# Split weights stored as interleaved high and low elements instead of in separate tiles

## What the reference computes

```
proj = (x * (1 + sc1) + sh1) @ w_in + b_in         # 2048 -> q, three kv, gates, r_x, r_y, merge gates
o_attn = attention(q, kv, gates) @ w_attn_o        # compressed, selected and window branches
o_rnn  = (rg_lru(conv(r_x)) * gelu(r_y)) @ w_rnn_o
mix = (g_attn * o_attn + g_rnn * o_rnn) @ w_out
x = layer_norm(ALPHA * x + (1 + g1) * mix)
gt, up = split((x * (1 + sc2) + sh2) @ w_ffn_in)   # 2048 -> 2 * 5632
x = layer_norm(ALPHA * x + (1 + g2) * ((silu(gt) * up) @ w_ffn_out))
```

## Time and profile before

| | |
|---|---|
| three runs | 1770.25, 1773.12, 1779.43 us; median 1773.12 |
| profiled execution | 1772.58 us, of which the span from first to last instruction is 1770.9 us |
| TensorE busy with matmuls | 1733.3 us, 13514 matmuls |
| weight loads | 1598.4 us, 13514 loads |
| DVE, ACT busy | 899.8 us, 710.9 us |
| mean granted TensorE clock | 0.994 |

### The profile page before, as it was taken

One profiled execution on the slowest core, in us unless ns is written; L12 is line 12 of the kernel. 1 busy time (PEld: TensorE's weight loads), 2 busy tenths in 40 slices (PEclk: granted clock), 3 DMA queues, 4 the chain that ended last, 5 costly groups with the idle time before them and its releaser, 6 DMA issues.

```text
span 1770.9 us, 34473 instructions
## 1 busy us (share of the span) xinstructions
PE 1733.3 (98%) x13514; PEld 1598.4 (90%) x13514; DVE 899.8 (51%) x1632; ACT 710.9 (40%) x1076; POOL 157.0 (9%) x271
## 2 busy tenths in 40 slices
PE   8989999999999999999999999999999999999997
PEld 3558888888999999889988899999999999999997
DVE  2233346755656655565873344444444444444565
ACT  2222236764545443343563333333333333333344
POOL 0001312203332311100000000000000000000001
PEclk9999999999999999999999999999999999999998
DMA  9998878757655647985647854545555444544542
GB/s 341 374 384 303 304 258 282 290 212 259 191 181 177 207 150 277 352 317 179 212 147 261 291 208 165 166 129 165 164 190 183 164 168 161 169 152 140 165 165 75
DMA packets 114152, 384.05 MB, mean 217 GB/s; under 512 B 14942, under 2 KB 15326, under 8 KB 113663
## 3 DMA queue, kind: packets, MB, share of 16 engines
q1 hardware_dynamic: 103248, 349.82, 57.1%
q0 software_dynamic: 10208, 32.32, 5.5%
q10 hardware_dynamic: 590, 0.44, 0.1%
HBM read 373.48 MB, written 9.03 MB: 216 GB/s over the span
## 4 chain that ended last, share of the span: by engine, by line
PE 91%; DMA 5%; DVE 1%; ACT 1%; issue 1%; SPq 0%; POOL 0%; POOLq 0%; ACTq 0%; DVEq 0%
PE bank L722 26%; PE bank L723 25%; PE bank L724 25%; DMA raw<-in_w_units 4%; PE bank L729 3%; PE bank L769 3%; PE bank L747 2%; PE bank L895 1%; PE bank L1015 1%; PE bank L931 1%; DMA mgate<-mg 0%; ACT z L1518 0%; PE bank L962 0%; DVE wlo L385 0%; SPq L486 0%
## 5 line engine op out<-in xcount | busy, mean ns | idle before, releaser
L722 PE MATMUL bank<-xhi,wlo 128*128 128x288 f32 x2544 | 756.9, 298 | 2.4 <-DVE wlo L385 1.7
L723 PE MATMUL bank<-xlo,whi 128*128 128x288 f32 x2544 | 750.2, 295 | 0.0
L724 PE MATMUL bank<-xhi,whi 128*128 128x288 f32 x2544 | 748.6, 294 | 0.0
L385 DVE TENSOR_TENSOR wlo<-raw,whi 128x1024 fp32r<-128x1024 f32 (+2 forms) x468 | 510.1, 1127 | 373.1 <-ACT whi L377 366.2
L377 ACT CAST whi<-raw 128x1024 fp32r<-128x1024 f32 (+2 forms) x468 | 434.0, 969 | 419.1 <-PE bank L724 272.7
L722 PEld LDWEIGHTS bank<-xhi,wlo 128*128 128x128 f32 x2544 | 477.7, 188 | 15.7 <-issue 13.8
L723 PEld LDWEIGHTS bank<-xlo,whi 128*128 128x128 f32 x2544 | 478.4, 188 | 0.6
L724 PEld LDWEIGHTS bank<-xhi,whi 128*128 128x128 f32 x2544 | 478.7, 188 | 0.0
L722 PE MATMUL bank<-hhi,wlo 128*128 128x288 f32 x704 | 208.5, 296 | 0.0
L723 PE MATMUL bank<-hlo,whi 128*128 128x288 f32 x704 | 208.0, 295 | 0.0
L724 PE MATMUL bank<-hhi,whi 128*128 128x288 f32 x704 | 207.5, 295 | 0.0
(11 more groups left out here) (332 smaller groups left out, 1680.3 us busy)
## 6 DMA issues: line engine op xcount, KB each, us to landing
raw<-in_w_units SPq DMA_DIRECT2D x556, 512.0 KB, 6.0
raw<-in_w_ffn_out_units SPq DMA_DIRECT2D x64, 384.0 KB, 3.0
raw<-in_w_ffn_out_units SPq DMA_DIRECT2D x64, 320.0 KB, 3.4
raw<-in_w_units SPq DMA_DIRECT2D x16, 448.0 KB, 8.4
mgate<-mg POOLq DMA_DIRECT2D x32, 144.0 KB, 4.1
mgl<-mgate POOLq DMA_DIRECT2D x16, 288.0 KB, 7.1
bz<-relrow POOLq DMA_DIRECT2D x16, 192.0 KB, 3.3
xt<-in_x SPq DMA_DIRECT2D x8, 288.0 KB, 7.2
```

The lines of the kernel that those rows point to most:

```text
L385: nc.vector.tensor_tensor(wlo[e][:, part], raw[:, s, spot], f32(whi[e][:, part]), ALU.subtract).then_inc(raw_used[s][h], 1)
L722: pe.matmul(acc, wt[1][:, w], x[0][:, c, :], start=start, stop=False)
L723: pe.matmul(acc, wt[0][:, w], x[1][:, c, :], start=False, stop=False)
L724: return pe.matmul(acc, wt[0][:, w], x[0][:, c, :], start=False, stop=stop)
```

## The change

The two tiles of a buffer become one, twice as long: `wsplit0` and `wsplit1`, seen as 2048 pairs. The high part of an element is the first of its pair, the low part the second. `whi` and `wlo` are now views of these tiles that take every second element.

```diff
-        whi = [behind(ctx, f"whi{e}", (0, 64)[e], UNIT) for e in range(2)]
-        wlo = [behind(ctx, f"wlo{e}", (64, 32)[e], UNIT) for e in range(2)]
-        xhi = tokens(ctx, "xhi", 96, DC)
+        wsplit = [behind(ctx, f"wsplit{e}", (0, 64)[e], 2 * UNIT).rearrange("p (n s) -> p n s", s=2) for e in range(2)]
+        whi, wlo = ([w[:, :, s] for w in wsplit] for s in range(2))
+        xhi = tokens(ctx, "xhi", 64, DC)
         xlo = tokens(ctx, "xlo", 0, DC)
```

## The result

The changed kernel takes 1783.5 us in the median of four runs (1780.35 to 1784.95), the kernel before 1773.1 us: 1.0052 times the time, with a 95% interval of 1.0029 to 1.0074. It is slower by half a per cent, where 3.3% faster was forecast. The profiled execution took 1780.35 us with a span of 1778.7 us, 7.8 us more than that of before.

The account below looks back on a forecast made before the run. TensorE's matmul pitch on the split products was taken as the bound. From 1772.6 us, 57.7 us gained (59.9 less 2.2) gave 1714.9 us, all other terms nothing; whole range 1665 to 1870 us.

Parts of the forecast that it names:

- Load beside columns: Split-product matmuls: a stepped load keeps its distance from the columns, removing 5.7 ns of each pitch, 57.7 us gained.
- two readers that get into each other's way: Split products: column stream and weight load disturb each other at certain address distances, making the pitch's excess.
- The 11.5 ns: Split-product matmuls: part of the 132.1 ns pitch beyond 120.6 ns of column streaming.
- rival 1: Split products: the excess is a fixed cost, pitch 132.1 +- 0.8 ns, time 1764 to 1781 us; chance 0.18.
- the plain columns: Line 931, plain float32: 0.838 ns a column against 0.833 for two cycles, taken as next to no excess beside loads.
- rival 2: Split products: loads touching twice the memory cost up to 11.5 ns more, 1833 us at half that; chance 0.31.
- The count of matmuls: Lines 722 to 724 and 729: 10944 matmuls touched, one nanosecond on all worth 10.9 us; 10512 counted.
- The load's cover: Split-product matmuls: a stepped load slower by less than 24 ns is hidden by the streaming.
- rival 3: Split products: the load becomes the bound from 132 ns on; at twice 108 ns, 2656 us; chance 0.04.
- The signs: Trace after, if right: 125 to 129 ns per matmul, loads still 188 ns, steps varying less, gain after 137 us.
- The offsets: Split tiles: some stay at multiples of 128 bytes, high and low share one distance from the tokens; not priced.
- cover of three microseconds: ACT and DVE splits: a unit takes 3.3 us, the matmuls between 6.3 us, so slower stepped writes were priced at nothing.

Follow-up runs that it names:

- c1: Kernel before, lines 722 to 724 streaming 256 of the 288 columns except at the first block of each sum; 1659.2 us.
- c5: Kernel before, lines 722 to 724 loading 64 of the 128 weight columns except at the first and last block of each sum; 1765.2 us.
- e1: Changed kernel, but high and low parts alternate by blocks of 128 elements in the shared tile, so loads have no step; 1774.9 us, ratio 1.0012.
- e4: Kernel before, with high and low parts of both buffers in one tile, so a load reads every fourth element; 2875.9 us, ratio 1.6224.
- e5: Kernel before, separate tiles without a step, all split weight and token tiles at a multiple of 128 bytes; 1781.5 us, ratio 1.0054.
- e3: Changed kernel with its step, xhi and xlo moved to 16 bytes behind a multiple of 128; 1781.4 us, ratio 1.0050.
- e6: Changed kernel with its step, the two split tiles moved to 32 and 16 bytes behind a multiple of 128; 1781.6 us, ratio 1.0056.
- e7: Changed kernel with its step, the two split tiles moved to 96 and 80 bytes behind a multiple of 128; 1784.85 us, ratio 1.0063.
- e2: Kernel before, separate tiles without a step, high and low tiles of a buffer at the same offset; 1768.75 us, ratio 0.9974.
- c3: Kernel before, lines 722 to 724 streaming 128 of the 288 columns except at the first block of each sum; 2206 us.
- c4: Changed kernel, lines 722 to 724 streaming 128 of the 288 columns except at the first block of each sum; 1748 us.

## Why the prediction was wrong

**The step that failed** is "Load beside columns", and ahead of it the reading of the 11.5 ns as "two readers that get into each other's way". From it came the one term of the sum, 57.7 us gained at 5.7 ns a matmul; measured are 1.25 ns lost on each of 7632, some 10 us. The 11.5 ns are no meeting of columns and load that a step could dissolve. They stay when columns go (c1: 119.6 ns, where columns plus 11 to 12 ns were to give 118.5 to 120) and when half of the load goes (c5: 131.4 ns, where sharing was to give 125 to 127), so they are nearly a fixed part of every such matmul, which was rival 1. I had let two rows with 0.14 us instead of 0.13 and a difference of 0.8 ns between stretches speak for the whole; they speak for one nanosecond. That the plain columns show no excess was no proof either: they are another kind of matmul (the four records at 267.84 us are two calls of line 931, two records each), and what is fixed in one need not be in the other.

**What does depend on places and steps** is 131.6 to 133.4 ns over all these kernels. The step's own share is 0.8 ns on `xhi`/`xlo` (133.4 in the change, 132.6 in e1), as far as e1 keeps the places, where rival 2 counted with 5.7 to 11.5: right in direction, far too large. Rival 1 had the mechanism, but its bound of 0.8 ns was too narrow for the sum: the step 0.8 and the places 0.5.

**What held.** The count of matmuls and what one nanosecond is worth: 9.5 us of loss from 1.25 ns on 7632 matmuls. The bound did not change: from 1010 to 1612 us PE is busy without a gap in both kernels. The load's cover held: 5 to 6 ns of the 18 to 24 were used. That rival 3 needs a load of 132 ns holds too, e4 shows it at 233. The signs did not: recorded loads were to stay at 188 ns and came to 195.

**Costs taken as nothing.** DVE's subtraction with a step costs nothing (1223 to 1225 ns). ACT's copy costs 10%; its cover of three microseconds held. The offsets got no term for want of a row. There was one to be had: in the trace of before, even units on `xhi`/`xlo` take 131.7 ns and odd ones 132.9 (the expectation of e5 has it), which is as much as the whole change.

**What stays open.** What the fixed 12 ns are; why a load with a step costs the matmul beside it 0.8 ns, while it is itself covered; whether a place exists where it doesn't (the change, e3, e6 and e7 put `xhi`/`xlo` at all eight multiples of 16 bytes within 128, and none brings the time back, but e2 and e5 show that the offset within 128 bytes isn't the whole of a place); and by which rule places without a step are good (e2) or bad (e5). e2 beats both kernels by 0.26% of the kernel before, but it was found, not derived.

## What to carry to other kernels

Before a layout is changed to remove a stall, show that the stall is one: take away columns, or half of the load, and see whether the pitch follows. With a step of two float32 elements, TensorE's loads, ACT's writes and DVE's reads and writes took 0 to 10% longer here; with a step of four, 1.7 to 2.1 times as long. A load that is covered can still cost the matmul beside it something, here 0.8 of 132 ns. Where every matmul has its own load, offsets of the tiles are worth measuring: e2 and e5 lie 0.8% apart in time (ratios 0.9974 and 1.0054), and no rule for them came out of these runs.

## What the runs showed that was not expected

With 128 columns per load and no step (c3), the granted clock fell to half at 998 us and stayed there to the end of the run; its earlier falls had lasted 24 us at most. Just before, until 996.3 us, PE had stood idle for 1.4 us, waiting for a split by DVE; from 1010 to 1500 us it was busy without a gap, and the clock did not rise. A window before and one behind:

```profile
960.00:996.00 36.00, 34.31 (x298) 29.46 (x297) 15.96 (x18) 17.10 (x25) 0.00 (x0) 1.00 0.89 316
...
1010.00:1500.00 490.00, 490.00 (x2277) 490.00 (x2277) 136.96 (x186) 105.18 (x140) 0.00 (x0) 0.50 0.31 102
```

At the lower level (1.2 GHz) a matmul of 128 columns takes 213.3 ns from start to start, against 111.7 at the higher one: the load, which sets this pitch, slows down with the clock. Loads with a step (c4) had such a stretch too, from 779 us on, behind a wait of 0.8 us, but were back at 1.00 at 953 us and kept it almost to the end, so that the kernel with the slower loads ended 458 us earlier. Each ran once; whether the clock would go the same way again is not shown.
